# A hybrid decoder layer: the HGRN chunk output from a block-diagonal state, and sample dots over 128 rows

## The reference, cut to what matters

```
S_t = diag(f_t) S_{t-1} + k_t i_t^T          o_t = S_t^T q_t
f = lb + (1 - lb) * sigmoid(hf);  k = 1 - f;  q = silu(hq)
```

## Time and profile before

| | |
|---|---|
| median of 3 runs | 988.9 us (987.56 to 989.34) |
| profiled execution: span, first to last instruction | 985.5 us |
| what the runs' median has around that span | 3.4 us |
| PE busy | 961.0 us (98%) |
| DVE, ACT, POOL busy | 526.4, 394.5, 237.7 us |
| mean granted TensorE clock, as a share of the full one | 0.990 |

### The profile page before, as it was taken

How to read it: one execution, slowest core, us unless ns; L and a number is a source line. 1 busy time by engine, 2 the same in 40 slices (tenths; PEclk the granted TensorE clock), 3 DMA queues, 4 the chain that set the end, 5 groups by cost and what they waited for, 6 DMA issues and landing times.

```text
span 985.5 us, 20971 instructions
## 1 busy us (share of the span) xinstructions
PE 961.0 (98%) x7866; PEld 928.7 (94%) x7866; DVE 526.4 (53%) x620; ACT 394.5 (40%) x524; POOL 237.7 (24%) x279
## 2 busy tenths in 40 slices
PE   7999999999999999999999999999999999999995
PEld 6999998898989999999999999999999999999994
DVE  5332275664754555456657656655566543435454
ACT  5443345363533544443325444444443321222333
POOL 0006075756501111000362111111111131212331
PEclk9999999999999999999999999999999999999998
DMA  7222422212113332353332332223223333322212
GB/s 233 65 86 86 172 76 65 75 35 71 53 53 108 101 90 85 106 188 110 94 97 76 91 102 85 85 87 104 86 85 105 101 93 106 91 85 80 73 36 92
DMA packets 168052, 91.49 MB, mean 93 GB/s; under 512 B 13584, under 2 KB 166560, under 8 KB 167600
## 3 DMA queue, kind: packets, MB, share of 16 engines
q1 hardware_dynamic: 149698, 80.61, 27.4%
q10 hardware_dynamic: 18320, 10.42, 3.7%
HBM read 83.10 MB, written 8.00 MB: 92 GB/s over the span
## 4 chain that ended last, share of the span: by engine, by line
PE 96%; ACT 1%; DVE 1%; DMA 1%; issue 1%; SPq 0%; ACTq 0%; DVEq 0%
PE acc L474 82%; PE lvb L556 3%; PE ob L605 1%; PE ob L606 1%; PE mb L628 1%; PE lvb L671 1%; DMA xtok<-in_x_prompt 1%; PE mb L683 1%; PE lvb L515 0%; PE mb L593 0%; PE mb L665 0%; PE ob L661 0%; PE ob L660 0%; PE lvb L642 0%; PE lvb L523 0%
## 5 line engine op out<-in xcount | busy, mean ns | idle before, releaser
L803 ACT ACTIVATE whi<-raw 128x1024 fp32r<-128x1024 f32 (+2 forms) x132 | 146.5, 1111 | 356.0 <-PE acc L474 354.9
L1123 DVE TENSOR_TENSOR wlo<-raw,whi 128x1024 fp32r<-128x1024 f32 (+2 forms) x132 | 193.2, 1464 | 178.9 <-ACT whi L803 178.9
L474 PE MATMUL acc<-xah,whi 128*128 128x260 f32 x896 | 188.0, 291 | 0.0
L474 PE MATMUL acc<-xah,wlo 128*128 128x260 f32 x896 | 181.5, 284 | 0.0
L474 PE MATMUL acc<-xal,whi 128*128 128x260 f32 x896 | 180.9, 284 | 0.0
L474 PE MATMUL acc<-xbh,whi 128*128 128x260 f32 x832 | 169.1, 284 | 3.2 <-DVE tg L1473 2.4
L474 PE MATMUL acc<-xbh,wlo 128*128 128x260 f32 x832 | 168.3, 284 | 0.0
L474 PE MATMUL acc<-xbl,whi 128*128 128x260 f32 x832 | 168.1, 284 | 0.0
L474 PEld LDWEIGHTS acc<-xah,whi 128*128 128x128 f32 x896 | 139.2, 190 | 8.9 <-issue 8.2
L474 PEld LDWEIGHTS acc<-xah,wlo 128*128 128x128 f32 x896 | 139.0, 190 | 0.0
L474 PEld LDWEIGHTS acc<-xal,whi 128*128 128x128 f32 x896 | 139.0, 190 | 0.0
(11 more groups left out here) (283 smaller groups left out, 1253.7 us busy)
## 6 DMA issues: line engine op xcount, KB each, us to landing
raw<-in_w_in SPq DMA_DIRECT2D x96, 256.0 KB, 3.1
raw<-in_w_up SPq DMA_DIRECT2D x88, 256.0 KB, 3.1
raw<-in_w_down SPq DMA_DIRECT2D x16, 384.0 KB, 3.3
raw<-in_w_down SPq DMA_DIRECT2D x16, 320.0 KB, 3.8
raw<-in_w_out SPq DMA_DIRECT2D x16, 256.0 KB, 2.9
raw<-in_w_ple_gate SPq DMA_DIRECT2D x8, 512.0 KB, 3.7
x_transposed<-xstg SPq DMA_DIRECT2D x1, 2080.0 KB, 7.5
hT<-x_transposed ACTq DMA_DIRECT2D x1, 2080.0 KB, 9.3
```

The costliest lines, as they stand in the source:

```text
L474: mm = pe.matmul(acc[tile % 2][:, b, 0:HT], wt[slot][:, w], xx[:, c, b * HT:(b + 1) * HT], start=first and i == 0 and q == 0, stop=last an ...
L803: act.activation(whi[k % 2][:, 0:n], raw[k % 2][:, 0:n], ACT.Copy).then_inc(hi_ready, 1)
L1123: dve.tensor_tensor(wlo[k % 2][:, 0:n], raw[k % 2][:, 0:n], whi[k % 2][:, 0:n].bitcast(fp), SUB).then_inc(lo_ready, 1)
```

## The change

- The state moves from `sst` to `sbd`, `[128, 4, 128]`, block-diagonal: the state of head 2c in partitions 0 to 63 and columns 0 to 63, that of head 2c+1 in partitions 64 to 127 and columns 64 to 127; the rest is zero. The helper `state(h2)` names one of the two blocks in all four groups.
- The chunk output is made by 4 matmuls of the whole array (state with queries, two heads at once), which now wait only for `ob`, and then, behind the waits for merges, `vst` and `mb`, by 8 matmuls of 128x64 tiles that add to it.
- DVE multiplies and adds the state in two halves of the partitions each.
- The sample dots run over all 128 rows, with a query `qz` that is zero on the other head's partitions; they alternate between the two halves, and PE's wait for itself is gone. DVE fills `qz` with two copies, where it filled `qs8` with one (in stage B).
- One buffer of `zq` lies on the retention state `rst` now, so POOL sets `rst` to zero after the last scores (again, where it did it at the start only).

```diff
-    sst = r("sst", [128, 4, 64])
+    sbd = r("sbd", [128, 4, 128])
+    qz = r("qz", [128, 2, NS])
...
-          for i, o in enumerate((T0 + 10400, r.at + 2048, r.at + 4096, T0 + 3 * TT * 4))]
+          for i, o in enumerate((T0 + 10400, r.at + 2048, r.at - 2048, T0 + 3 * TT * 4))]
...
+        def state(h2):
+            return sbd[64 * h2:64 * h2 + 64, :, 64 * h2:64 * h2 + 64]
...
+                pe.wait_ge(o_free, it + 1)
+                for c in range(4):
+                    pe.matmul(ob[:, c * 128:(c + 1) * 128], sbd[:, c, :], lq[3][:, c, :], start=c == 0, stop=False)
                 pe.wait_ge(merged, it * MERGES + (MERGES + 1))
                 pe.wait_ge(vst_ready, it + 1)
-                pe.wait_ge(o_free, it + 1)
                 wait_misc(M_B, 3, it, 6)
                 for h in range(8):
-                    out = ob[64 * (h % 2):64 * (h % 2) + 64, (h // 2) * 128:(h // 2 + 1) * 128]
-                    pe.matmul(out, vst[:, h * 64:(h + 1) * 64], sfull[:, h, :], start=True, stop=False)
-                    mm = pe.matmul(out, head(sst, h), head(lq[3], h), start=False, stop=True)
+                    mm = pe.matmul(ob[64 * (h % 2):64 * (h % 2) + 64, (h // 2) * 128:(h // 2 + 1) * 128],
+                                   vst[:, h * 64:(h + 1) * 64], sfull[:, h, :], start=False, stop=h >= 6)
...
-                for h2 in range(2):
-                    for b in range(NS):
-                        mm = pe.matmul(mb[64 * h2:64 * h2 + 64, b:b + 1], ss[64 * h2:64 * h2 + 64, b, :],
-                                       qs8[64 * h2:64 * h2 + 64, b:b + 1], start=True, stop=True)
-                    if h2 == 0:
-                        step(mm)
+                for b in range(NS):
+                    for h2 in range(2):
+                        mm = pe.matmul(mb[64 * h2:64 * h2 + 64, b:b + 1], ss[:, b, :], qz[:, h2, b:b + 1],
+                                       start=True, stop=True)
...
+                    dve.tensor_copy(qz[0:64, 0, :], q[0:64, it, NT:TT])
+                    dve.tensor_copy(qz[64:128, 1, :], q[64:128, it, NT:TT]).then_inc(smp_staged, 1)
                 else:
                     dve.tensor_copy(ks8[:], k[:, it, NT:TT])
-                dve.tensor_copy(qs8[:], q[:, it, NT:TT]).then_inc(smp_staged, 1)
+                    dve.tensor_copy(qs8[:], q[:, it, NT:TT]).then_inc(smp_staged, 1)
...
-                step(dve.tensor_tensor(sst[:], sst[:], tl[LV][:].broadcast_to([128, 4, 64]), MUL))
+                for h2 in range(2):
+                    mine = slice(64 * h2, 64 * h2 + 64)
+                    step(dve.tensor_tensor(state(h2), state(h2), tl[LV][mine].broadcast_to([64, 4, 64]), MUL))
                 dve.wait_ge(misc_full, it * 6 + (M_B + 4))
-                dve.tensor_tensor(sst[:], sst[:], mb[:, 0:256].rearrange("p (c v) -> p c v", c=4),
-                                  ADD).then_inc(misc_free, 1)
+                for h2 in range(2):
+                    mine = slice(64 * h2, 64 * h2 + 64)
+                    grown = dve.tensor_tensor(state(h2), state(h2),
+                                              mb[mine, 0:256].rearrange("p (c v) -> p c v", c=4), ADD)
+                grown.then_inc(misc_free, 1)
...
-            for t, v in ((ones128, 1.0 / 128), (ones1024, 1.0 / DM), (eps, EPS), (ssx, 1.0), (sst, 0.0), (rst, 0.0), (one, 1.0)):
+            for t, v in ((ones128, 1.0 / 128), (ones1024, 1.0 / DM), (eps, EPS), (ssx, 1.0), (sbd, 0.0), (qz, 0.0), (one, 1.0)):
...
             pool.wait_ge(v_taken, 17)
+            pool.wait_ge(sc_full, 4 * LV)
+            pool.memset(rst[:], 0.0)
```

More of the change, by code:

```diff
@@ L327, in hybrid_layer @@
         stored = sem("stored")
-        pe_s, act_s, dve_s, pool_s = (sem(n) for n in ("pe_step", "act_step", "dve_step", "pool_step"))
+        act_s, dve_s, pool_s = (sem(n) for n in ("act_step", "dve_step", "pool_step"))
         pe_passed, act_passed, dve_passed, pool_passed = (
@@ L445, in taken @@
                 pe.sem_inc(pe_passed, 1)
-            step = Steps(pe, pe_s, taken)
             def level(n):
@@ L538, in _ @@
                         v_transposes()
-            def head(t, h, cols=slice(None)):
-                return t[64 * (h % 2):64 * (h % 2) + 64, h // 2, cols]
             def scores(use, it):
@@ L566, in _ @@
             with pe.Fori(0, 4) as it:
-                step.loop(it, 1)
                 def first_scores():
@@ L625, in _ @@
                 taken()
-                for h2 in range(2):
-                    for b in range(NS):
-                        mm = pe.matmul(mb[64 * h2:64 * h2 + 64, b:b + 1], ss[64 * h2:64 * h2 + 64, b, :],
-                                       qs8[64 * h2:64 * h2 + 64, b:b + 1], start=True, stop=True)
-                    if h2 == 0:
-                        step(mm)
+                for b in range(NS):
+                    for h2 in range(2):
+                        mm = pe.matmul(mb[64 * h2:64 * h2 + 64, b:b + 1], ss[:, b, :], qz[:, h2, b:b + 1],
+                                       start=True, stop=True)
                 mm.then_inc(misc_full, 1)
-            step.end(4)
             pe.wait_ge(v_taken, 17)
@@ L988, in _ @@
                 act.dma_start(hg_prompt[0, 0].rearrange("(c two) k v -> two k c v", two=2)[h2],
-                              sst[64 * h2:64 * h2 + 64]).then_inc(stored, 16)
+                              state(h2)).then_inc(stored, 16)
             act.dma_start(ret_prompt[0, 0].rearrange("h d v -> d h v"), rst[:]).then_inc(stored, 16)
@@ L1255, in _ @@
             with dve.Fori(0, 4) as it:
-                step.loop(it, 6)
+                step.loop(it, 7)
                 dve.wait_ge(misc_free, it * 6 + M_B)
```

## The result

The changed kernel takes 967.31 us (median of 4 runs, 966.45 to 967.89), the kernel before 989.12 on the same chip (987.56 to 989.47). The ratio is 0.9782, with a 95% interval of 0.977 to 0.9794: 21.8 us faster where 19.3 were forecast. The span of the profiled execution is 966.1; the forecast for it was 966.2.

A forecast was written before the change was run, and what follows sets the result against it. PE, busy 98% of the span, was taken to bound the kernel. Outputs 15.9 plus dots 3.4 save 19.3 us, taking span 985.5 to 966.2; adding 3.4 gives a median of 969.6 us, range 966 to 975.

The forecast's parts named there:

- The output matmuls: Stage B chunk output on PE: 1.92 us, khat starting 3.97 us earlier a round, 15.9 in four.
- The dots: Stage B sample dots on PE: 1.10 us instead of 2.23; gains only in rounds 1 to 3, 3.4 together.
- The wait that takes their place: PE before the scores, rounds 0 to 2: new wait of about 1 us on zq, 5.53 from dots to scores.
- VectorE: State multiply and add in two halves: 2.1 us, hidden before PE's head squares with 0.7 us to spare.
- The merge: VectorE's second merge before PE's next scores: delayed by an extra 0.1 copy, nothing shows, no more than 0.35 slack.
- The clock: Half clock behind dots stretched rounds 1 and 2, which gain 1.21 and 1.10; a fall there now is hidden by zq.
- the term that carries the span over to the median: Whole kernel: the runs' median stands 3.4 us above the profiled span, added to 966.2.
- (a): Rival on PE's outputs and dots: column halves don't overlap for long streams or loads; 975.1 us, chance 0.12.
- (b): Rival: clock falls elsewhere, in dense stretches, 1.7 us each; 973.0 us for two rounds, 976.4 for four; chance 0.12.
- (c): Rival: ScalarE's zq is not late, so dots give 1.1 in three more places; 966.2 us, chance 0.06.
- (d): Rival: slower, each change of column half on PE costs like a change of tile shape; 991.3 us, chance 0.02.

The follow-up runs named there:

- e3: Kernel before with only its 16 output matmuls reordered, first the eight 128x64 tiles, then the eight 64x64; 973.41 us, ratio 0.9846.
- e4: Changed kernel with column halves not alternating: outputs all even heads then odd, dots one half then the other; 972.21 us, ratio 0.9825.
- e7: Changed kernel with sample dots over 64 rows, alternating halves, without PE's wait for itself; 966.94 us, ratio 0.9781 to the kernel before.
- e2: Kernel before with only the sample dots changed (128 rows, masked queries, alternating halves, no PE wait for itself); 984.03 us, ratio 0.9956.
- e1: Changed kernel with the sample dots and `qs8` staging taken back, so only the outputs changed; 971.16 us, ratio 0.9832 to the kernel before.
- e6: Changed kernel plus ScalarE padding the next chunk's first two query levels earlier and VectorE merging before its staging; 963.43 us, ratio 0.9745.
- e5: Changed kernel plus only ScalarE padding the next chunk's first two query levels earlier; 975.79 us, ratio 0.9856 to the kernel before.

## Why the prediction was right

- **The output matmuls.** Forecast 1.92, measured 1.91. e3 shows that the alternation of shapes and not the 64-row tile was what cost, and e4 that the overlap of halves is real, though what it is worth depends on what stands behind in the queue. Neither measures a change of shape by itself. The rows nearest to that are e3's, where eight 128x64 tiles with a change behind them take 1.03 and the changed kernel's eight without one take 0.93: 0.10, where the prediction had 0.14. Two slips of the prediction left the sum alone. The 64 + 64 that it calls matmuls are the recorded instructions, 32 + 32 matmuls in four rounds; and the wait of 0.1 for the bank may have been a change of shape.
- **The dots.** Forecast 1.10 from L609's row, measured 1.06. But e7 shows the same 1.1 with 64 rows, so neither the mask nor the 128 rows made it. Two things did: e4 has neither PE's wait for itself nor the alternation, and its dots take 1.75. So some 0.5 of the 1.17 go with the wait (no run drops it alone; that the halves overlap at their border in e4 is in it too), and 0.7 with the alternation. The dots' gain (3.4 forecast, 3.5 in e2's stage B) is of two kinds: 1.2 in round 3, and 2.3 in rounds 1 and 2, where what went is two falls of the clock.
- **The wait that takes their place.** Forecast a wait of about 1 on zq in three rounds and 5.53 from dots to scores; measured 1.3 and 5.5. Dots to dots 38.6 to 38.8 was forecast, 38.71 measured. In round 0 the dots gave nothing: e1, with long dots, has 38.71 there as well, and e2 has the 42.70 of before. The wait is real and not a mere re-labelling: e6 takes 3.9 us out by removing it with what lies behind it.
- **VectorE.** Two multiplies and two adds had been put at 2.1 us, with 0.7 to spare. DVE's rows, and PE's head squares:

```profile
150.88 1.19 DVE L1286 TENSOR_TENSOR sbd<-sbd,tl 64x256 f32<-64x256 f32 x2
152.19 0.85 DVE L1290 TENSOR_TENSOR sbd<-sbd,mb 64x256 f32<-64x256 f32 x2
...
153.82 1.02 PE L616 MATMUL mb<-sq,cst 128*128 128x512 f32 x2
```

  They end at 153.04, 2.16 after they begin, and the head squares start at 153.82: 0.8 to spare, and no wait.
- **The merge** was said to have no more than 0.35 of slack. The changed kernel has 0.15 (the merge ends at 166.94 + 1.33 = 168.27, the scores start at 168.42). That is why e5 could gain nothing; that it lost 8.5 took the longer staging and the falls of the clock as well.
- **The clock** fell behind two of the four dots before and not in stage B of the changed kernel, in the profiled execution; it did in e1 and e3, whose dots are long. The prediction had the gain of rounds 1 and 2 (1.21 and 1.10) from the stretched half products, and said that a fall in the same place would cost nothing now, as zq hides it. The second half was not put to the test, for no fall came there. Which rounds the clock falls in is not explained here: it fell behind 2 of before's four dots of 2.2 us and behind 1 of e1's.
- **What was off: 2.5 us of 21.8**, in the term that carries the span over to the median. I had added 3.4. In all runs of this case the time is 1.8 above the execution's own span; the 3.4 came of setting a median of runs against the span of one execution. That execution was a short one for before: its span of 985.5 at a clock of 0.990 is that of the fastest of all runs of before on record (987.25 us), and the typical run had a clock of 0.988. The changed kernel's own runs show 0.993 to 0.995. A mean clock lower by 0.002 is some 2 us of span, as an estimate (0.004 of 987 us more at half clock, of which half is lost). In spans, before's median run is 989.12 - 1.8 = 987.3, 1.8 above its profile, and the changed kernel's is 965.5, 0.6 below its profile. These 2.4 us are the difference between 19.4 in the profiled pair and 21.8 in medians. That the spans came out to 0.1 is right for stage B (19.3) and luck for the rest, where single falls of the clock come and go.
- **The rivals.** (a), halves that don't overlap, is refuted by the rows and e4. (b) did not come about in the changed kernel; e5 shows its price, about 1.5 us a fall (1.7 forecast). (c) is refuted by the 5.5 us. (d) is refuted: a change of half costs nothing, it gains.

## What to carry to other kernels

Before restructuring data so that small matmuls fill the array, sort them by tile shape and alternate the column halves: here the order alone, with PE's wait for itself dropped, gave 19.5 us in medians where the whole change gave 21.8. When an edit shortens work that stands before a wait, list the next two things that come just in time, and move them together; moving only the first cost 8.5 us here. And carry a profiled span over to a median only with the gap between one run's own time and its span.

## What the runs showed of the hardware

- fp32 matmuls of 128 columns that alternate between 128x64 and 64x64 tiles start 0.361 us apart (before), full-array ones 0.222. A single change between the two shapes costs about 0.10 (1.03 for eight tiles in e3 against 0.93 in the changed kernel).
- Matmuls of one column start 0.06 us apart per instruction in one tile (e4: 32 in 1.82) and 0.03 apart if they alternate between column halves (32 in 1.10), with the weights over 64 or 128 rows alike. The rule of the Trainium skill that the prediction quotes ("TensorE: Matmul & The Clock Gate", Part 3, The mechanism: a weight load overlaps with matmuls in flight only if its row group differs) would not have this for 128 rows, where all tiles share their rows.
- Matmuls into two different banks, the last outputs and the first khat, overlap as well when they lie in different column halves (e4).
- Operations of 8 columns on VectorE took 0.6 to 0.7 us beside a row of GpSimd operations without a pause (e5), and 0.2 to 0.3 where GpSimd had just paused (changed kernel).
- In this case the granted clock fell to 1.2 GHz behind 7 of 16 dots of 2.2 us and behind all three waits of 2.6 us, but never in stage B behind dots of 1.1 us with a wait of 1.3 us three microseconds later. A fall cost 1.1 to 1.5 us.
